# Decode stage of a hybrid trunk: separate step lists for three engines, another bank for the token turns, page numbers read before the buffer's wait

## The chip, the cores and the metric

One core of a Trainium2 chip runs the whole program in one launch. The metric is the device time in microseconds, median of several runs. All arithmetic is float32.

## The reference

Two layers over a prompt of 1024 tokens and 8 decode rows. Each layer projects once and splits the columns among three groups: latent attention (4 heads), an RWKV-7 time mixing (4 heads of 64, a 64x64 state per head) and a gated mixing of chunks. What matters here is the decode attention and the prompt's RWKV recurrence:

```python
# decode attention: 8 samples, 32 pages of 128 tokens each, latent width 256, rotary width 64
s_past = (einsum('blhr,bpr->bhlp', q_abs, ckv_past) + einsum('blhd,bpd->bhlp', q_pe, kpe_past)) * ATTN_SCALE
p = softmax(concatenate([s_past, s_new], -1))
o_lat = einsum('bhlp,bpr->blhr', p[..., :P], ckv_past) + einsum('bhlm,bmr->blhr', p[..., P:], ckv)

# RWKV-7, prompt: 1024 steps, run in the kernel as 16 chunks of 64
sa = einsum('bhvk,bhk->bhv', S, kk_t)
S = S * d_t - sa * b_t + v_t * k_t
o_t = einsum('bhvk,bhk->bhv', S, r_t)
```

The pages are gathered from a pool of 320 by `page_table`.

## The kernel before, in words

Each layer is a series of stages; the change is in one of them, the decode stage (lines 1328 to 1858). It does two independent things at once: the decode attention over the 8 samples' caches, and the chunked RWKV recurrence of the prompt. The engines have their own programs and meet at semaphores; each executes its program strictly in order.

**Attention.** A half-sample h (0 to 15, `NH`) is two page blocks q = 2h, 2h+1 of 8 pages each (`qpage`). The buffer holds six blocks (`QS`), that is three half-samples. SP loads a block with `load(sp, q)`: `reg_load` reads eight page numbers from the table into registers (line 401), and eight DMAs of 160 KB follow (line 404). From block 6 on SP first waits for `pg_free`, which TensorE raises when PV has read the block that lay there. For each h there are ten steps rb of 32 columns (`NB`): VectorE transposes the pages' columns in 32x32 blocks into one of four slots (`turn`, "T" below, line 1748), TensorE multiplies them with the queries in 32x32 tiles ("S", line 1589, 16 matmuls' passes). Then VectorE takes the maximum ("MX", lines 1807 to 1815), ScalarE the exponential ("EX", line 1690), TensorE transposes the probabilities into bank 4 ("PT", line 1598), ScalarE copies them out in four pieces (line 1700), and TensorE adds P V into bank 7 ("PV", line 1607). T waits for the step four before it to be used (`kt_used`), and for rb = 0 for its pages.

**Recurrence.** A pair p of chunks goes with the half-samples 2p and 2p+1. `prepare(p, n)` needs nothing of the state: MA and AK build the products inside a chunk; X1, Y1 to X5, Y5 invert a triangular 64x64 matrix in five levels (TensorE X, a copy of ScalarE, TensorE Y, an addition and a transpose of VectorE, then the next X; all in 32x32 tiles in bank 5); TA and TB transpose the token rows (b, k and v) in bank 6, from where ScalarE copies them. `follow(p - 1, n)` carries the state of the pair before: Z, U, H for each chunk c = 0, 1 and OO for the output, all in bank 6, each waiting for a copy or an addition of the one before. Z, U, H, OO and MA, AK are in 64x64 tiles, PT, TA, TB in 128x128, PV in 128x32.

**The order.** One list, `plan`, is written out by rule and walked by TensorE, ScalarE and VectorE alike; each picks the entries that concern it. "T" has no entries of its own: VectorE turns step n + 2 where the list has S of step n. For a pair the list gives TensorE this order (first digit of S: the half-sample of the pair; PT- and PV- belong to the half-sample before the pair):

```
S00 S01 MA Z0 S02 S03 PT- X1 U0 S04 S05 PV- Y1 H0 S06 S07 X2 Z1 S08 S09 Y2 U1 X3
S10 S11 H1 Y3 S12 S13 PT0 OO X4 S14 S15 PV0 AK Y4 S16 S17 TA X5 S18 S19 TB Y5
```

MX0 and EX0 stand between Y2, U1 and X3, MX1 and EX1 around Y5. TA waits for `ak_done`, because both use bank 6, and TB for `ta_done`.

Of the kernel before, what the change touches and what calls it, by code (L numbers as in the profile page):

```python
# [99 lines left out]
def bass_hybrid_trunk(nc, a):  # L100
    with ExitStack() as ctx:
# [92 lines left out]
        with nc.Fori(0, DEPTH) as layer:  # L194
# [198 lines left out]
            sv_io = sem("sv_io")  # L393
            pg_in = [sem(f"pg_in{i}") for i in range(QS)]
            HB = (10328, 0, 5120)
            tab = lnb[0:1, 0:NS * PAGES].bitcast(I32)
            qpage = lambda q: RB[:, HB[q // 2 % 3] + q % 2 * QW:HB[q // 2 % 3] + (q % 2 + 1) * QW].rearrange("p (s c) -> p s c", c=KW)

            def load(sp, q):
                regs = [sp.alloc_register(f"page{q}_{j}") for j in range(8)]  # L400
                sp.reg_load(regs, tab[:, 8 * q:8 * q + 8])
                for j, r in enumerate(regs):
                    page = sp.snap(r, donate=True)
                    sp.dma_start(qpage(q)[:, j], a["cache"][lay, bass.ds(page, 1), :, 0:KW].rearrange("l o p c -> (l o p) c")).then_inc(pg_in[q % QS], 16)
# [135 lines left out]
            with nc.Block() as block:  # L540
# [517 lines left out]
                def _(dve):  # L1058
# [229 lines left out]
                    for what, n, x in plan:  # L1288
# [40 lines left out]
            s_kn = sem("s_kn")  # L1329
            pg_free = sem("pg_free")  # L1330
            kt_used = sem("kt_used")
# [71 lines left out]

            STEPS = ["MA", "Z0", "X1", "U0", "Y1", "H0", "X2", "Z1", "Y2", "U1", "X3", "H1", "Y3", "OO",
                     "X4", "AK", "Y4", "TA", "X5", "TB", "Y5"]
            chain = ("Z", "U", "H", "O")


            plan = []
            for h in range(NH):  # L1410
                mine = [("rw", n) for n in (STEPS[0:11] if h % 2 == 0 else STEPS[11:])]
                for rb in range(0, NB, 2):
                    plan += [(h, "S", rb), (h, "S", rb + 1)]
                    if rb == 2 and h:
                        plan.append((h - 1, "PT", 0))
                    if rb == 4 and h:
                        plan.append((h - 1, "PV", 0))
                    if rb < 8:
                        plan += [(h // 2, *mine.pop(0)), (h // 2, *mine.pop(0))]
                rest = [(h // 2, *x) for x in mine]  # L1420
                plan += rest[:1] + [(h, "MX", 0)] + rest[1:2] + [(h, "EX", 0)] + rest[2:]
            plan += [(NH - 1, "PT", 0), (NS, "rw", "Z0"), (NH - 1, "PV", 0), (0, "FC", 1), (NS, "rw", "U0"), (0, "FC", 2), (NS, "rw", "H0"),
                     (0, "FC", 3), (NS, "rw", "Z1"), (0, "FC", 4), (NS, "rw", "U1"), (0, "FC", 5), (NS, "rw", "H1"), (0, "FC", 6),
                     (NS, "rw", "OO")]

            with nc.Block() as block:
                @block.sync
                def _(sp):
# [23 lines left out]
                def _(pe):  # L1452
# [4 lines left out]
                    def prepare(p, n):  # L1457
# [19 lines left out]
                        elif n == "TA":  # L1477
                            pe.wait_ge(ak_done, p + 1)
                            for f in range(2):
                                pe.transpose(PB[:, 6, f * P:(f + 1) * P], A2[:, f, p * P:(p + 1) * P], ident)  # L1480
                            for f in range(2):
                                mm = pe.transpose(PB[:, 6, (2 + f) * P:(3 + f) * P], pT[:, 2 + f, p * P + 1:(p + 1) * P + 1], ident)
# [43 lines left out]
                    def follow(p, n):  # L1526
# [45 lines left out]

                    for h, what, g in plan:
                        if what == "rw" and g[0] in chain:
# [58 lines left out]
                def _(act):  # L1633
                    def prepare(p, n):
# [9 lines left out]
                        elif n == "TA":  # L1644
                            act.wait_ge(ta_full, p + 1)
                            t6 = PB[:, 6, :].rearrange("p (v f w k) -> p v f w k", v=2, f=2, w=2)
                            for c in range(2):
                                for w in range(2):
                                    op = act.activation(TOK[k][hp[w], 0:2, 2 * c:2 * c + 2, :], t6[hp[c], :, :, w, :], ACT.Identity)
                            op.then_inc(ta_done, 1)  # L1650
# [27 lines left out]

                    for h, what, g in plan:
                        if what == "rw" and g[0] in chain:  # L1680
# [57 lines left out]
                def _(dve):  # L1738
# [20 lines left out]
                    def prepare(p, n):  # L1759
                        k = p % 2  # L1760
                        B = PB[:, 5, :].rearrange("p (v d c) -> p v d c", v=2, d=4)
                        if n == "MA":
# [9 lines left out]
                            dve.drain()  # L1772
                            dve.transpose(Tm.rearrange("p d c -> p (d c)"), Tc.rearrange("p d c -> p (d c)")).then_inc(tm_done, 1)
                            levels(2, LEVELS).then_inc(bm_done, 1)
                        elif n == "AK":
                            dve.wait_ge(ak_full, p + 1)
# [20 lines left out]
                    for h, what, g in plan:  # L1797
# [386 lines left out]
```

## Time and profile before

| what | value |
|---|---|
| median of 3 runs | 2040.42 us (2036.16 to 2041.38) |
| profiled execution, its own time | 2037.07 us |
| its span | 2035.4 us |
| TensorE busy | 1865.2 us (92%) |
| VectorE busy | 895.6 us (44%) |
| ScalarE busy | 494.7 us (24%) |
| page loads (line 404) | 512 of 160 KB, 2.6 us median from issue to landing |
| first and last S (line 1589) | 625.0 to 1871.6 us |

The busy shares are over the whole program. In the 40 slices of the page (51 us each) the decode stage lies in slices 13 to 17 for layer 0 and 33 to 37 for layer 1, where VectorE's digits are 6 to 7 and the DMA queues move 150 to 190 GB/s. A matmul's end is modelled, and float32 matmuls appear as two instructions each, so that one S group (8 matmuls) is 16 rows of the trace.

### The profile page before, as it was taken

The numbers are of one execution on the slowest core, as the hardware profiler recorded it, in microseconds if no ns is written. First come the engines' busy times: TensorE is split into PE (matmuls) and PEld (weight loads), VectorE is DVE, ScalarE is ACT, GpSimd is POOL, SyncE is SP. The second block draws the span as 40 slices with busy tenths as digits, with TensorE's granted clock in tenths as the row PEclk, the third lists the DMA queues.
The fourth block names the chain that finished last, engine by engine and source line by source line (L and its number), as shares of the span: only waits on it lengthen the run. The fifth ranks groups of instructions, "written<-read, shape, count | busy, mean of one in ns | idle before, by whom it ended". The sixth has DMA issues, their size and how long they took to land. (4 is left out here: it accounts for less than half of the span.)

```text
span 2035.4 us, 45818 instructions
## 1 busy us (share of the span) xinstructions
PE 1865.2 (92%) x19360; PEld 1164.3 (57%) x19360; DVE 895.6 (44%) x1984; ACT 494.7 (24%) x1164; POOL 172.6 (8%) x158
## 2 busy tenths in 40 slices
PE   4899999999987999899949999999999879998898
PEld 2565676666654666654326656766666546665543
DVE  2024134222766676654230340332318577775542
ACT  3111012222412333311131110222224123333201
POOL 0010000011334000000000100000212240000000
PEclk9899999999999999979989999999999899999899
DMA  9500000000205666341075001010001166562411
GB/s 388 207 11 27 21 21 32 21 21 13 59 26 159 185 188 180 109 178 42 32 301 213 0 27 32 11 32 22 21 22 50 28 186 186 176 186 83 178 42 42
DMA packets 103927, 191.18 MB, mean 94 GB/s; under 512 B 17162, under 2 KB 87260, under 8 KB 100004
## 3 DMA queue, kind: packets, MB, share of 16 engines
q1 hardware_dynamic: 103716, 188.19, 27.9%
q8 instruction: 154, 2.52, 0.5%
q14 instruction: 57, 0.47, 0.1%
HBM read 175.41 MB, written 21.19 MB: 97 GB/s over the span
## 5 line engine op out<-in xcount | busy, mean ns | idle before, releaser
L771 PE MATMUL PB<-RB,R 128*128 128x344 f32 x1632 | 496.1, 457 | 0.0
L771 PEld LDWEIGHTS PB<-RB,R 128*128 128x128 f32 x1632 | 303.7, 191 | 159.6 <-issue 19.7
L1946 PE MATMUL PB<-RB,R 128*128 128x512 f32 x512 | 221.2, 593 | 0.0
L1589 PE MATMUL PB<-WUQ,Q 32*32 32x256 f32 x5120 | 191.0, 385 | 14.7 <-DVE WUQ L1748 9.4
L1748 DVE STREAM_TRANSPOSE WUQ<-RB 128x512 f32<-128x512 f32 x316 | 197.0, 676 | 5.5 <-DMA RB<-in_cache 5.3
L1946 PEld LDWEIGHTS PB<-RB,R 128*128 128x128 f32 x512 | 97.0, 190 | 120.8 <-issue 118.6
L931 ACT ACTIVATE R<-PB 128x344 f32<-128x344 f32 x90 | 41.2, 457 | 423.4 <-PE PB L771 423.4
L1184 DVE TENSOR_TENSOR PB<-PB,CST 128x128 f32<-128x128 f32 x64 | 18.8, 294 | 226.3 <-PE PB L791 226.3
L1589 PEld LDWEIGHTS PB<-WUQ,Q 32*32 32x32 f32 x5120 | 90.0, 104 | 46.0 <-DVE WUQ L1748 23.1
L619 PE MATMUL PB<-RB,R 128*128 128x344 f32 x288 | 88.5, 472 | 10.8 <-PEq L225 10.8
L619 PEld LDWEIGHTS PB<-RB,R 128*128 128x128 f32 x288 | 57.1, 199 | 41.4 <-issue 14.8
L246 PE MATMUL PB<-R,WUQ 128*32 128x512 f32 x192 | 33.5, 667 | 49.2 <-DMA R<-in_w_ada 49.2
L1066 DVE COPY R<-PB 128x320 f32<-128x320 f32 x16 | 7.9, 491 | 149.7 <-PE PB L630 149.7
L788 PE MATMUL PB<-RB 128*128 128x128 f32 (+2 forms) x192 | 71.5, 495 | 0.0
L630 PE MATMUL PB<-RB 128*128 128x320 f32 x256 | 69.2, 432 | 0.0
L1607 PE MATMUL PB<-RB 128*32 128x256 f32 x1024 | 67.4, 404 | 1.9 <-ACT RB L1700 1.9
L2041 POOL TENSOR_TENSOR sm<-sm,small 128x1 f32<-128x1 f32 (+1 forms) x18 | 9.9, 550 | 698.6 <-DVE sm L2073 698.6
L942 ACT ACTIVATE R<-PB,sm,small 128x128 f32<-128x128 f32 (+3 forms) x64 | 53.2, 832 | 56.8 <-DVE sm L1188 56.2
L760 PE MATMUL PB<-R,RB 128*128 128x256 f32 x256 | 61.1, 383 | 0.0
L630 PEld LDWEIGHTS PB<-RB 128*128 128x128 f32 x256 | 48.6, 190 | 20.3
L1700 ACT ACTIVATE RB<-PB 64x256 f32<-64x256 f32 x128 | 48.3, 378 | 39.1 <-PE PB L1598 37.8
L2015 ACT ACTIVATE RB<-PB 128x1024 f32<-128x1024 f32 x16 | 16.3, 1021 | 161.2 <-PE PB L1946 161.2
(355 smaller groups left out, 2619.6 us busy)
## 6 DMA issues: line engine op xcount, KB each, us to landing
RB<-in_cache SPq DMA_DIRECT2D x512, 160.0 KB, 2.6
R<-in_w_ada SPq DMA_DIRECT2D x16, 1536.0 KB, 17.4
R<-in_w_in SPq DMA_DIRECT2D x44, 512.0 KB, 3.7
RB<-in_w_out SPq DMA_DIRECT2D x8, 1024.0 KB, 9.9
RB<-out_x_stream SPq DMA_DIRECT2D x2, 4096.0 KB
out_x_stream<-RB SPq DMA_DIRECT2D x16, 512.0 KB
RB<-in_x_prompt SPq DMA_DIRECT2D x1, 4096.0 KB
RB<-in_w_kv SPq DMA_DIRECT2D x2, 1280.0 KB, 5.6
```

Source lines behind the costliest of these rows:

```text
L619: mm = pe.matmul(bigbank(n)[:, c, :], ring[:, i % 4, k, :], hT[:, k, c * CH:(c + 1) * CH], start=(k == 0), stop=(k == KT - 1))
L630: mm = pe.matmul(smlbank("kv", t)[:, 0:KVW], hT[:, k, cols(t)], wkv_in[:, k, :], start=(k == 0), stop=(k == KT - 1))
L760: mm = pe.matmul(jobbank(j)[:, 0:256].rearrange("p (w c) -> p w c", w=2), hT[:, k, cols(c)], w2, start=(k == 0), stop=(k == KT - 1))
L771: mm = pe.matmul(jobbank(j)[:, 0:CH], ring[:, blkno[n] % 4, k, :], hT[:, k, chunk(c)], start=(k == 0), stop=(k == KT - 1))
L788: pe.matmul(sbank(2 * u + e)[:, c:c + w], qT[:, h, i * P:(i + 1) * P], kT[:, h, c:c + w], start=True, stop=False)
L931: act.activation(to, jobbank(j)[:, 0:CH], fn).then_inc(pj_free[j % 2], 1)
L942: act.activation(pbuf(n), sbank(n), ACT.Exp, bias=nbr[:, n:n + 1], scale=scq[:, i:i + 1], accum_out=Lr[:, n:n + 1]).then_inc(ex_done, 1)
L1589: mm = pe.matmul(PB[qp[o], 2 * (h % 2) + q % 2, 0:256], Q4[qp[q], g, :], k[qp[q], c], start=(g == 0), stop=(g == NB - 1), skip_group_check ...
L1607: mm = pe.matmul(PB[qp[c], 7, f * KVL:(f + 1) * KVL], PT[:, s, 32 * c:32 * c + 32], qpage(q)[:, (4 * s + c) % 8, RP:RP + KVL], start=(h == ...
L1700: op = act.activation(PT[hp[w], :, e * 64:(e + 1) * 64], t4[hp[e], :, w, :], ACT.Identity)
L1748: op = dve.transpose(KTr[:, n % 4], pages[:, :, fcol(rb):fcol(rb) + 32])
L1946: mm = pe.matmul(PB[0:n, 2 * (t % 2) + hf, :], mixT[:, k, cols(t)], wo[:, k, hf * 512:(hf + 1) * 512], start=(k == 0), stop=(k == 5))
```

## The change

SP's `load` reads the page numbers first and waits for the buffer afterwards. The common `plan` is replaced by a list for each engine, written out as words and expanded over the pairs. The word T gives VectorE's turns places of their own; LV is the second part of MA's levels, D a drain, and G0 and G1 are the scaling of the state for the next chunk, taken out of H0 and H1, with drains only in the last pair. Z0 now stands ahead of MA, PT- stands between U0 and H0, X1 stands behind PV-, S groups stand alone at seven places, and TB stands ahead of X5. TA's transposes go to bank 4, where the probabilities are turned, and no longer to bank 6: TA waits for `pp_done` of the pair's first half-sample, PT of the odd half-sample waits for `ta_done`, TB for `ak_done`, and Z also for `ta_done`.

```diff
-            def load(sp, q):
+            def load(sp, q, freed=0):
                 regs = [sp.alloc_register(f"page{q}_{j}") for j in range(8)]
                 sp.reg_load(regs, tab[:, 8 * q:8 * q + 8])
+                if freed:
+                    sp.wait_ge(pg_free, freed)
...
+            chain = ("Z", "U", "H", "G", "O")
+            PE_PAIR = (
+                "S00 S01 Z0 MA U0 PT- S02 H0 S03 S04 PV- X1 S05 Y1 S06 S07 Z1 S08 S09 U1 X2 S10 H1 Y2 S11 PT0 S12 OO "
+                "X3 PV0 Y3 S13 S14 S15 X4 AK TA Y4 S16 S17 TB S18 X5 S19 Y5"
+            ).split()
+            DVE_PAIR = (
+                "T02 T03 T04 MA T05 T06 H0 LV T07 T08 T09 Y1 T10 MX0 T11 G0 T12 D H1 Y2 T13 T14 T15 G1 T16 Y3 T17 T18 "
+                "T19 AK Y4 T20 T21 MX1"
+            ).split()
+            ACT_PAIR = (
+                "Z0 U0 PT- MA X1 Z1 U1 X2 EX0 PT0 OO X3 X4 TA X5 TB Y5 EX1"
+            ).split()
...
                     for q in range(4, 2 * NH):
-                        if q >= QS:
-                            sp.wait_ge(pg_free, q - QS + 1)
-                        load(sp, q)
+                        load(sp, q, max(q - QS + 1, 0))
...
                         elif n == "TA":
-                            pe.wait_ge(ak_done, p + 1)
+                            pe.wait_ge(pp_done, 2 * p + 1)
                             for f in range(2):
-                                pe.transpose(PB[:, 6, f * P:(f + 1) * P], A2[:, f, p * P:(p + 1) * P], ident)
+                                pe.transpose(PB[:, 4, f * P:(f + 1) * P], A2[:, f, p * P:(p + 1) * P], ident)
...
                         elif n == "TB":
-                            pe.wait_ge(ta_done, p + 1)
+                            pe.wait_ge(ak_done, p + 1)
...
                         if n[0] == "Z":
+                            pe.wait_ge(ta_done, p + 1)
                             pe.wait_ge(tb_done, p + 1)
...
                             if h:
                                 pe.wait_ge(pp_done, h)
+                            if h % 2:
+                                pe.wait_ge(ta_done, h // 2 + 1)
...
+                        elif n[0] == "G":
+                            i = 2 * p + int(n[1])
                             if i + 1 < NCH:
-                                dve.drain()
+                                if p == NS - 1:
+                                    dve.drain()
                                 dve.tensor_tensor(Sg, S0[:, (i + 1) % 4], ecol[:, :, i + 1:i + 2].broadcast_to([P, 2, 64]), ALU.mult)
-
-                    for h, what, g in plan:
+                                if p == NS - 1:
+                                    dve.drain()
+
+                    for h, what, g in pair_plan(DVE_PAIR):
...
-                        elif what == "S":
-                            if NB * h + g + 2 < NB * NH:
-                                turn(NB * h + g + 2)
+                        elif what == "T":
+                            turn(NB * h + g)
```

`pair_plan(words)` expands the words for p = 0 to 7, drops what lies outside the half-samples, and appends `TAIL`, the same end as before with G0 added behind H0.

## Rows read from the trace of the kernel before

**Rows 1.** Timeline of TensorE, 743 to 776 us: start, length, work, idle before it.
```profile
744.44 1.09 PE L1467 MATMUL PB<-RB 64*64 64x128 f32 x16 [0.45 <-ACT R L1661]
...
746.95 0.66 PE L1598 MATMUL PB<-CST,grow 128*128 128x128 f32 x4
748.01 0.45 PE L1515 MATMUL PB<-RB 32*32 32x32 f32 x32 [0.41 <-DVE RB L1773]
748.40 0.45 PE L1549 MATMUL PB<-RB,R 64*64 64x64 f32 x8
...
750.26 1.93 PE L1607 MATMUL PB<-RB 128*32 128x256 f32 x32
...
752.51 0.33 PE L1556 MATMUL PB<-R 64*64 64x64 f32 x4
...
753.12 1.09 PE L1589 MATMUL PB<-WUQ,Q 32*32 32x256 f32 x32
754.01 0.54 PE L1515 MATMUL PB<-RB 32*32 32x32 f32 x32
...
756.44 0.45 PE L1549 MATMUL PB<-RB,R 64*64 64x64 f32 x8
757.30 0.45 PE L1515 MATMUL PB<-RB 32*32 32x32 f32 x32 [0.42 <-DVE RB L1783]
757.58 1.14 PE L1589 MATMUL PB<-WUQ,Q 32*32 32x256 f32 x32
758.66 0.33 PE L1556 MATMUL PB<-R 64*64 64x64 f32 x4
...
759.77 0.45 PE L1522 MATMUL PB<-RB 32*32 32x32 f32 x32 [0.29 <-ACT RB L1664]
...
761.12 0.66 PE L1598 MATMUL PB<-CST,grow 128*128 128x128 f32 x4
761.71 0.33 PE L1565 MATMUL PB<-R 64*64 64x64 f32 x4
...
771.17 0.44 PE L1487 MATMUL PB<-CST,R 128*128 128x128 f32 x2 [0.35 <-ACT R L1649]
...
771.81 1.14 PE L1589 MATMUL PB<-WUQ,Q 32*32 32x256 f32 x31
773.40 1.09 PE L1467 MATMUL PB<-RB 64*64 64x128 f32 x16 [0.45 <-ACT R L1661]
```

**Rows 2.** Timeline of TensorE's weight loads: the second S group ahead of PV.
```profile
749.66 0.18 PEld L1589 LDWEIGHTS PB<-WUQ,Q 32*32 32x32 f32 x16 [0.41 <-DVE WUQ L1748]
```

**Rows 3.** Timeline of VectorE: the end of the first pair, then a pair's start.
```profile
650.46 1.30 DVE L1748 STREAM_TRANSPOSE WUQ<-RB 128x512 f32<-128x512 f32 x2 [2.20 <-DMA RB<-in_cache]
...
742.24 0.65 DVE L1808 TENSOR_REDUCE sm<-PB 128x1 f32<-128x512 f32 x1
...
743.72 1.29 DVE L1748 STREAM_TRANSPOSE WUQ<-RB 128x512 f32<-128x512 f32 x2
745.58 0.35 DVE L1764 TENSOR_SCALAR RB<-PB,CST 128x128 f32<-128x128 f32 x1 [0.56 <-PE PB L1467]
...
748.32 2.48 DVE L1748 STREAM_TRANSPOSE WUQ<-RB 128x512 f32<-128x512 f32 x4
```

**Rows 4.** Timeline of ScalarE in the same pair.
```profile
754.61 0.28 ACT L1664 ACTIVATE RB<-PB 128x128 f32<-128x128 f32 x1 [4.95 <-PE PB L1515]
...
759.45 0.27 ACT L1664 ACTIVATE RB<-PB 128x128 f32<-128x128 f32 x1
...
773.25 0.68 ACT L1690 ACTIVATE grow<-PB,sm 128x512 f32<-128x512 f32 x1
```

**Rows 5.** SP: lengths of line 404 and 401 (min/median/max ns), and waits, 640 to 880 us.
```profile
L404 SPq DMA_DIRECT2D RB<-in_cache x512: 332/333/1782, 547.8 to 1849.9; - x171
L401 SPq TENSOR_LOAD <-lnb x64: 520/525/772, 546.8 to 1844.2; - x64
SPq L401 <- PE PB L1607: 27.9, 12, 3.5
```

**Rows 6.** Windows behind the stage: TensorE, loads, VectorE, ScalarE, GpSimd, clock, DMA share, GB/s.
```profile
880.00:900.00 20.00, 18.00 (x69) 12.75 (x68) 7.99 (x19) 6.19 (x10) 0.00 (x0) 0.69 0.91 354
```

More of the change, by code:

```diff
@@ L394, in bass_hybrid_trunk @@
             pg_in = [sem(f"pg_in{i}") for i in range(QS)]
+            pg_free = sem("pg_free")
             HB = (10328, 0, 5120)
@@ L1329, in bass_hybrid_trunk @@
             s_kn = sem("s_kn")
-            pg_free = sem("pg_free")
             kt_used = sem("kt_used")
@@ L1402, in bass_hybrid_trunk @@
             fcol = lambda rb: RP + 32 * rb if rb < 8 else 32 * (rb - 8)
[L1404 to L1421, printed above, removed]
@@ L1422, in bass_hybrid_trunk @@
-            plan += [(NH - 1, "PT", 0), (NS, "rw", "Z0"), (NH - 1, "PV", 0), (0, "FC", 1), (NS, "rw", "U0"), (0, "FC", 2), (NS, "rw", "H0"),
-                     (0, "FC", 3), (NS, "rw", "Z1"), (0, "FC", 4), (NS, "rw", "U1"), (0, "FC", 5), (NS, "rw", "H1"), (0, "FC", 6),
-                     (NS, "rw", "OO")]
+            chain = ("Z", "U", "H", "G", "O")
[3 more added lines that the diff above has]
+            ).split()
@@ new lines, in bass_hybrid_trunk, with pair_plan @@
+            DVE_PAIR = (
[5 more added lines that the diff above has]
+            ).split()
+            def pair_plan(words):
+                out = []
+                for p in range(NS):
+                    for w in words:
+                        if w[0] in "ST" and w[1] in "012":
+                            out.append((2 * p + int(w[1]), w[0], int(w[2])))
+                        elif w[:2] in ("PT", "PV", "MX", "EX"):
+                            out.append((2 * p - 1 if w[2] == "-" else 2 * p + int(w[2]), w[:2], 0))
+                        else:
+                            out.append((p, "rw", w))
+                return [x for x in out if 0 <= x[0] < NH] + TAIL
@@ L1426, in bass_hybrid_trunk @@
+            TAIL = [(NH - 1, "PT", 0), (NS, "rw", "Z0"), (NH - 1, "PV", 0), (0, "FC", 1), (NS, "rw", "U0"), (0, "FC", 2), (NS, "rw", "H0"),
+                    (NS, "rw", "G0"), (0, "FC", 3), (NS, "rw", "Z1"), (0, "FC", 4), (NS, "rw", "U1"), (0, "FC", 5), (NS, "rw", "H1"),
+                    (0, "FC", 6), (NS, "rw", "OO")]
             with nc.Block() as block:
@@ L1477, in prepare @@
                         elif n == "TA":
-                            pe.wait_ge(ak_done, p + 1)
+                            pe.wait_ge(pp_done, 2 * p + 1)
                             for f in range(2):
-                                pe.transpose(PB[:, 6, f * P:(f + 1) * P], A2[:, f, p * P:(p + 1) * P], ident)
+                                pe.transpose(PB[:, 4, f * P:(f + 1) * P], A2[:, f, p * P:(p + 1) * P], ident)
                             for f in range(2):
-                                mm = pe.transpose(PB[:, 6, (2 + f) * P:(3 + f) * P], pT[:, 2 + f, p * P + 1:(p + 1) * P + 1], ident)
+                                mm = pe.transpose(PB[:, 4, (2 + f) * P:(3 + f) * P], pT[:, 2 + f, p * P + 1:(p + 1) * P + 1], ident)
                             mm.then_inc(ta_full, 1)
                         elif n == "TB":
-                            pe.wait_ge(ta_done, p + 1)
+                            pe.wait_ge(ak_done, p + 1)
                             for f in range(2):
@@ L1571, in follow @@
                             mm.then_inc(oo_full, 1)
-                    for h, what, g in plan:
+                    for h, what, g in pair_plan(PE_PAIR):
                         if what == "rw" and g[0] in chain:
@@ L1645, in prepare @@
                             act.wait_ge(ta_full, p + 1)
-                            t6 = PB[:, 6, :].rearrange("p (v f w k) -> p v f w k", v=2, f=2, w=2)
+                            t4 = PB[:, 4, :].rearrange("p (v f w k) -> p v f w k", v=2, f=2, w=2)
                             for c in range(2):
                                 for w in range(2):
-                                    op = act.activation(TOK[k][hp[w], 0:2, 2 * c:2 * c + 2, :], t6[hp[c], :, :, w, :], ACT.Identity)
+                                    op = act.activation(TOK[k][hp[w], 0:2, 2 * c:2 * c + 2, :], t4[hp[c], :, :, w, :], ACT.Identity)
                             op.then_inc(ta_done, 1)
@@ L1677, in follow @@
                             act.activation(A3[:, :, p * P:(p + 1) * P], PB[:, 6, 0:2 * P].rearrange("p (f t) -> p f t", f=2), ACT.Identity).then_inc(oo_done, 1)
-                    for h, what, g in plan:
+                    for h, what, g in pair_plan(ACT_PAIR):
                         if what == "rw" and g[0] in chain:
@@ L1773, in prepare @@
                             dve.transpose(Tm.rearrange("p d c -> p (d c)"), Tc.rearrange("p d c -> p (d c)")).then_inc(tm_done, 1)
+                        elif n == "LV":
                             levels(2, LEVELS).then_inc(bm_done, 1)
+                        elif n == "D":
+                            dve.drain()
                         elif n == "AK":
@@ L1792, in follow @@
                             op.then_inc(st_done, 1)
+                        elif n[0] == "G":
+                            i = 2 * p + int(n[1])
                             if i + 1 < NCH:
-                                dve.drain()
+                                if p == NS - 1:
+                                    dve.drain()
                                 dve.tensor_tensor(Sg, S0[:, (i + 1) % 4], ecol[:, :, i + 1:i + 2].broadcast_to([P, 2, 64]), ALU.mult)
-                    for h, what, g in plan:
+                                if p == NS - 1:
+                                    dve.drain()
+                    for h, what, g in pair_plan(DVE_PAIR):
                         if what == "rw" and g[0] in chain:
```

## The prediction

> **What bounds the kernel now.** I read the page first (busy shares, the 40 slices), then the waits between 640 and 880 us, then the timelines of TensorE, VectorE and ScalarE over one pair of half-samples, 744 to 773 us, where nothing of the start or the end of the stage mixes in. The reader is to see there that the decode stage (about 625 to 881 us in layer 0, 1635 to 1893 us in layer 1) repeats one pattern eight times per layer. Its period is the distance between two MA groups on TensorE: 773.40 - 744.44 = 28.96 us [rows 1]. TensorE executes its own list in order, and its groups follow each other without a hole except at a few places; ScalarE has a pause of 4.95 us in it [rows 4] and VectorE another while it waits for Y1 and AK. So the stage is TensorE's work plus the holes that the order of its list makes.
>
> I price the holes from start to start, against the same group where it does not wait [rows 1]. (a) S18 S19 and then Y5, S00, S01 up to MA: 771.81 to 773.40 is 1.59 us, two S groups ahead of a 64x64 group normally take 758.66 - 757.58 = 1.08, so 0.51. (b) PT: 748.01 - 746.95 = 1.06 against 761.71 - 761.12 = 0.59, so 0.47. (c) U0 S04 S05: 750.26 - 748.40 = 1.86 against 1.08 and a U of 0.38, so 0.40 (no U is seen without a wait: I take it between half an H, 0.31, and its own duration, 0.45). (d) U1: 757.30 - 756.44 = 0.86 against 0.38, so 0.48. (e) H1: 759.77 - 758.66 = 1.11 against 753.12 - 752.51 = 0.61, so 0.50. (f) TB: idle 0.35 us for TA's copies, as its row says. Sum 2.71 us, and the work without holes is 28.96 - 2.71 = 26.25 us.
>
> **The change part by part.** The matmuls, copies and transposes of a pair stay the same in number, shape and operands; only their order, TA's bank and some waits differ. So TensorE's 26.25 us stay, apart from the seams. Two S groups take 754.01 - 753.12 = 0.89 us in front of another 32x32 group, 0.445 each, and a lone S in front of PV, a group of another tile size, takes 750.26 - 749.66 = 0.60 [rows 1, 2]. The difference, 0.15, is a seam. Counting the runs of 32x32 groups (S, X, Y) that end in another size, the old order has 12 per pair and the new one 11: work 26.10 us.
>
> The Trainium skill ("TensorEngine Tiling (Array Packing)", Tiling Modes, Key Properties) says that each change of tiling mode drains the engine, so by it every change of size counts, also 64x64 to 128x128. That would be 26 changes before and 24 after, another 0.15 us per pair, some 2 us over the kernel; the rows here price only exits from 32x32, and I keep to them.
>
> Now the new holes. I walk the new lists with X5 of a pair's end at 0, with these prices: one turn T 2.48/4 = 0.62; MX to the next instruction 743.72 - 742.24 = 1.48; MA with its levels 748.32 - 745.58 = 2.74 [rows 3]; a copy of X 0.28 and EX 0.68 with some 0.1 for its sum [rows 4]; the other groups by their start distances in the same timeline of TensorE (Z 0.57, MA 0.93, PV 1.86, OO 1.54, AK 1.02, TA 0.59, TB 0.36).
> - X5 to Y5. X5's result is there after 0.5, its copy ends at 0.85, Y5 can start at 0.9; S19 between them covers up to about 0.6. Hole 0.3 (before, TA's copies stood in front of X5's).
> - S00 S01 at 1.15, Z0 at 2.2, MA at 2.8. MA wants the copy after Y5, which ScalarE does behind TB's four copies: ready at 2.6. Hole (a) goes, because Z0 now stands in front of MA. Late next is z_done for U0: ScalarE's Z0 copy now stands behind EX1, which waits for MX1, which waits for S19 (done at 0.85). 0.9 + 1.55 + 0.05 + 0.78 + 0.05 + 0.28 gives 3.6 and U0 wants it at 3.7. No hole, but only 0.1 of cover; without it every tenth counts.
> - U0, PT, S02, H0, S03, S04, PV. H0's copy of U0 is covered by PT and S02 (1.2 us against 0.85). PT's four copies end at 6.3, PV starts at 6.95. VectorE does T02 to T04, MA, T05, T06: MA's transpose is out at 6.6 and X1, moved behind PV, wants it at 8.8. Holes (b) and (c) go.
> - X1, S05, Y1. One S (0.45) and X1 itself cover 0.7 of 0.9: hole 0.2.
> - S06 S07 Z1 S08 S09 U1 X2 S10 H1 Y2 S11. Y1's transpose is out at 11.15, X2 wants it at 13.05: hole (d) goes. S10 and H1 (1.2 us) cover X2's copy: hole (e) goes. MX0 waits for S09 (12.8); T11 behind it is out at 15.0 and S11 wants it at 14.8: hole 0.2.
> - PT0 S12 OO X3 PV0. EX0's result at 15.2 and PT0 at 15.6; H1's state is out at 16.3 (behind MX0, T11, G0, T12) and OO wants it at 16.8; X3 at 18.3 has Y2's transpose since 16.8; PT0's copies end at 17.9, PV0 starts at 18.8. No hole.
> - Y3 S13 S14 S15 X4 AK TA Y4 S16 S17 TB S18. Y3's transpose is out at 21.9, X4 wants it at 22.2. TA's bank is free since 17.9. TB's wait on AK ends at 24.4, wanted at 25.6; TB no longer waits for TA's copies (the rest of f). X5 wants Y4's transpose (25.5) at 26.4. No hole.
> Added waits on TensorE (ta_done in front of both Z groups and of the odd PT) are long satisfied. Their cost isn't in the trace; between 0 and the 0.05 us that lies between the end of a releasing copy and the group that it releases (the copy of L1664 for Y3 ends at 759.45 + 0.27 and Y3 starts at 759.77, [rows 1, 4]) I take 0.05 each, 0.15 a pair. Taking the drains out of VectorE's G steps gives less than 0.2 us on an engine that has 3 us of pauses left: nothing.
>
> New period: 26.10 + 0.3 + 0.2 + 0.2 + 0.15 = 26.95 by the sum, in which X5's and Y5's own time is partly counted twice with their holes, and 26.4 by adding the starts of the walk directly. I take 26.6, between them: 2.36 us less per pair.
>
> **The page loads.** SP issues 32 loads a pair. One issue is 0.33 us and now and then up to 1.78; a read of eight page numbers takes 0.52, and SP waits 27.9 us for PV in layer 0, in 12 of the waits [rows 5]. So the two bursts of 16 fill 28.96 - 27.9/8 = 25.5 us of a pair, 12.7 each. In the new order PV- frees its first buffer at 7.9, the burst ends at 20.6 and the pages land 2.6 later (the median in the page's list of loads), 23.2; T20 wants them at 25.4. PV0 frees at 19.8, behind the first burst at 20.6: landed at 35.9, which is 9.3 of the next pair against T10 at 11.1. About 2 us of cover both times. Reading the numbers ahead of the wait takes 0.5 us off each even burst, behind that cover: worth nothing while it lasts.
>
> **Start and end of the stage.** T20 of the first pair waits for page block 5 until 650.46 [rows 3], and block 5 is issued without waiting for any buffer. The first pair cannot end earlier: gain 0. The tail behind the last S19 is a chain (MX, EX, PT, copies, PV, the final combination) with the same steps: 0, with two drains more, under 0.2. So seven pairs per layer gain, 14 x 2.36 = 33 us.
>
> **Sum.** The profiled execution took 2037.07 us (span 2035.4). 2037.1 - 33 = 2004.1. The median of the timed runs stands 3.35 us above the profiled one, so I forecast 2007.4, about 2007 us, 1.6% less.
>
> **Rivals.**
> 1. The page loads become the bound. For: SP is busy 25.5 of 28.96 us, more than any other engine but TensorE, and bursts without their pause would fill 25.5 of the new 26.6. Against: 1.1 us is left, and landing has 2 us. If each issue's queueing grows so that a burst takes 13.6 us, the period is 27.2 and the gain 14 x 1.75 = 25 us: 2016.
> 2. The seams eat the gain. The new list has seven lone S groups where the old has none; I priced them by one row. If each costs 0.2 more (a full new fill, half of S's own 0.44), 1.4 us of the 2.36 goes: 14 x 0.96 = 13 us, 2027.
> 3. Slower than before. MX now stands in front of things that TensorE wants next, at two places: MX1, EX1, Z0's copy for U0 (cover 0.1) and MX0, T11 for S11 (none). A delay d of the maxima costs 2d a pair; from d = 1.2 us the gain is gone, and at 1.48 us (VectorE held up in front of it by as much as one more MX) the kernel is 14 x 0.6 = 8 us slower: 2048. Against it: MX starts within 0.1 us of its last S today.
> 4. The clock. TensorE's granted clock is 0.69 between 880 and 900 us [rows 6], that is between its levels of 1.2 and 2.4 GHz, behind the tail of the stage, in which TensorE mostly waits. Where the low stretch falls on the projection it costs time at half speed; shifted by a few us in each layer it can give or take 5 us. This widens the range of every case and is not a case of its own.
>
> **Numbers.** Forecast 0.62 (own range 1998 to 2016); rival 1 0.12; rival 2 0.15; rival 3 0.05; 0.06 for all holes closed (14 x 2.71 = 38 us, 2002, and with the clock below 1998). Within 0.3% (6 us, about what runs of this kernel can tell from no change) lies the upper part of rival 2 and the start of 3: 0.07. Range 1998 to 2024. Faster 0.88, same 0.07, slower 0.05.
>
> **What would show it.** In the profile after: the MA distance near 26.6 us in the middle of the stage; no idle of TensorE in front of MA, X3, Y3 or TB; small idle in front of Y5, Y1 and S11; VectorE never idle for DMA behind the first pair; SP's waits for PV down to some 10 us a layer. The forecast is wrong if U0 or S11 waits for over 0.5 us a pair, if a lone S takes over 0.7 us, or if VectorE waits for pages in several pairs.

## The result and the profile after

The changed kernel takes 2014.93 us (median of 4 runs) against 2040.90 us for the kernel before: the ratio is 0.9875, 95% interval 0.9852 to 0.9897, so 26 us or 1.25% less. A second group of runs gave 2014.23 us against 2039.85 us (0.988, 0.9851 to 0.9908). Forecast were 2007 us and 33 us less; the direction and the range held, and a fifth of the gain is missing. One of the first four runs took 2745.53 us, in the slow state of the chip (granted clock 0.65 instead of 0.97); it is left out of the ratio, though not of the median.

The profiled execution has a span of 2012.6 us, 22.8 less than before. Of these the decode stage gives 18.0: from its first S to its last, it was 234.3 us in layer 0 and 236.7 in layer 1, and is 225.6 and 227.4. The remaining 4.8 us lie in stages that the change doesn't touch, 2.6 of them before the stage of layer 0 begins: the first S stands at 622.4 instead of 625.0 us, with the same matmuls at a mean granted clock of 0.99 instead of 0.98. I don't count them for the change. Of the 33 us forecast for the stage, the one profile shows 18, then, and the timed runs some 21 to 26.

Busy rows of the page after, TensorE, its loads, VectorE and ScalarE, are nearly those of before, as they must be:

```profile
PE 1864.4 (93%) x19360; PEld 1165.3 (58%) x19360; DVE 896.8 (45%) x1984; ACT 497.4 (25%) x1164; POOL 172.1 (9%) x158
```

The distances between the MA groups of TensorE (the period that the forecast put at 26.6 us) are, in us:

```
pair            1->2   2->3   3->4   4->5   5->6   6->7   7->8
before, layer 0 26.35  33.77  29.32  28.94  28.96  30.29  29.44
after,  layer 0 27.84  32.20  27.25  28.10  29.06  28.84  26.25
before, layer 1 26.89  35.14  29.27  28.93  29.44  30.09  29.75
after,  layer 1 28.97  30.45  31.08  29.40  28.56  26.25  26.69
```

Two things stand there. Where nothing disturbs it, the new order runs at 26.25 us, even less than the walk's 26.4. And most pairs don't reach it: from the third on, seven of ten periods lie between 27.3 and 31.1 us. The forecast had asked for 26.6 us in the middle of the stage; that sign did not appear.

Here is the undisturbed pair, from the timeline of TensorE after (Z0 in front of MA, then as in the list):

```profile
796.73 1.04 PE L1475 MATMUL PB<-RB 64*64 64x128 f32 x16
797.61 0.40 PE L1558 MATMUL PB<-RB,R 64*64 64x64 f32 x8
797.93 0.66 PE L1609 MATMUL PB<-CST,grow 128*128 128x128 f32 x4
798.52 0.66 PE L1598 MATMUL PB<-WUQ,Q 32*32 32x256 f32 x16
799.11 0.33 PE L1565 MATMUL PB<-R 64*64 64x64 f32 x4
...
802.88 0.72 PE L1598 MATMUL PB<-WUQ,Q 32*32 32x256 f32 x16
803.47 0.45 PE L1530 MATMUL PB<-RB 32*32 32x32 f32 x32
...
806.83 0.45 PE L1523 MATMUL PB<-RB 32*32 32x32 f32 x32
807.11 0.72 PE L1598 MATMUL PB<-WUQ,Q 32*32 32x256 f32 x16
...
808.37 0.45 PE L1530 MATMUL PB<-RB 32*32 32x32 f32 x32
808.90 0.67 PE L1598 MATMUL PB<-WUQ,Q 32*32 32x256 f32 x16
...
814.47 0.45 PE L1530 MATMUL PB<-RB 32*32 32x32 f32 x32
814.75 1.58 PE L1598 MATMUL PB<-WUQ,Q 32*32 32x256 f32 x48
...
818.12 0.45 PE L1530 MATMUL PB<-RB 32*32 32x32 f32 x32
818.40 1.15 PE L1598 MATMUL PB<-WUQ,Q 32*32 32x256 f32 x32
819.47 0.44 PE L1495 MATMUL PB<-CST,R 128*128 128x128 f32 x2
...
820.32 0.32 PE L1502 MATMUL PB<-RB 32*32 32x32 f32 x10
...
822.47 0.33 PE L1547 MATMUL PB<-R 64*64 64x64 f32 x4
```

Between these rows TensorE never stands idle long enough for the trace to name a releaser. The lone S (02) takes 799.11 - 798.52 = 0.59, as [rows 2] had it. Two of the three holes that the forecast left show as slack from start to start: S05 to Y1 is 0.59 where an S in a run is 0.445 (0.15, forecast 0.2), Y2 to S11 is 0.53 where Y1 to S06 is 0.27 (0.26, forecast 0.2). The third, 0.3 in front of Y5, can't be read by itself, because X5, S19 and Y5 overlap in the trace; from X5 to Z0 it is 822.47 - 820.32 = 2.15, and 2.2 in the walk.

And here a disturbed pair, 738.8 to 767.9 us, 2.8 us longer:

```profile
749.24 0.33 PE L1523 MATMUL PB<-RB 32*32 32x32 f32 x16
749.84 0.33 PE L1523 MATMUL PB<-RB 32*32 32x32 f32 x16 [0.28 <-issue]
750.02 0.67 PE L1598 MATMUL PB<-WUQ,Q 32*32 32x256 f32 x16
...
757.28 0.43 PE L1530 MATMUL PB<-RB 32*32 32x32 f32 x27
758.06 0.22 PE L1530 MATMUL PB<-RB 32*32 32x32 f32 x3 [0.35 <-issue]
758.08 0.43 PE L1598 MATMUL PB<-WUQ,Q 32*32 32x256 f32 x5
...
761.50 0.38 PE L1530 MATMUL PB<-RB 32*32 32x32 f32 x23
762.34 0.23 PE L1530 MATMUL PB<-RB 32*32 32x32 f32 x4 [0.45 <-issue]
762.38 0.40 PE L1598 MATMUL PB<-WUQ,Q 32*32 32x256 f32 x1
...
763.41 0.44 PE L1495 MATMUL PB<-CST,R 128*128 128x128 f32 x2
...
766.36 1.08 PE L1598 MATMUL PB<-WUQ,Q 32*32 32x256 f32 x28 [0.42 <-issue]
767.37 0.33 PE L1547 MATMUL PB<-R 64*64 64x64 f32 x4
```

The reader is to see that TensorE stops inside its groups. X2 is one group of 32 instructions with waits only ahead of its first; its first 16 start at 749.24, the rest at 749.84, and the idle is "issue": nothing that the profile shows was waited for. From start to start against the undisturbed pair: X2 to S10 0.78 instead of 0.28, Y3 to S13 0.80 instead of 0.28, Y4 to S16 0.88 instead of 0.28, TB to Z0 3.96 instead of 3.00. These four breaks are 2.58 of the 2.81 us.

TensorE's instructions have a queue of their own on the page (q8, by its size). Of the page after, queues with packets, MB and share:

```profile
q1 hardware_dynamic: 103716, 188.19, 28.4%
q8 instruction: 154, 2.52, 0.5%
q14 instruction: 57, 0.47, 0.1%
```

154 packets for TensorE's 38,720 matmuls and loads are one for about 251 of them, 16 KB each. A pair has some 1,730, so seven refills a pair, one in 3.8 us at the new pace. That the breaks are refills that come late was a theory at this point.

The trace bears it out. These are TensorE's matmuls and loads from one resumption to a later one in the disturbed pair (the stretch, TensorE, loads, VectorE, ScalarE, GpSimd, clock, DMA share, GB/s):

```profile
749.84:758.06 8.22, 7.87 (x255) 5.22 (x256) 5.59 (x16) 3.23 (x9) 0.00 (x0) 1.00 0.67 194
758.06:762.34 4.28, 3.83 (x129) 3.05 (x130) 3.07 (x6) 1.00 (x3) 0.00 (x0) 1.00 0.57 169
762.34:766.36 4.02, 3.60 (x127) 1.82 (x128) 2.80 (x8) 2.37 (x10) 0.00 (x0) 1.00 0.81 241
```

That is 511, 259 and 255 instructions, two blocks of 256, one and one (what overlaps an edge counts on both sides). Numbered through in the order of their starts, waits included, 16 of the 17 gaps of over 0.35 us inside a group in pairs 3 to 6 of both layers stand at a multiple of 256 from one another within their layer. At each of the 22 block ends with a gap of over 0.25 us TensorE goes on 1.2 to 1.6 us after a 16 KB packet of q8 has ended.

The second loss is at the start. VectorE's waits for pages, in the timelines of VectorE after (first two pairs of layers 0 and 1):

```profile
647.62 1.30 DVE L1759 STREAM_TRANSPOSE WUQ<-RB 128x512 f32<-128x512 f32 x2 [3.84 <-DMA RB<-in_cache]
664.86 0.71 DVE L1759 STREAM_TRANSPOSE WUQ<-RB 128x512 f32<-128x512 f32 x1 [3.49 <-DMA RB<-in_cache]
```
```profile
1648.42 1.30 DVE L1759 STREAM_TRANSPOSE WUQ<-RB 128x512 f32<-128x512 f32 x2 [5.43 <-DMA RB<-in_cache]
1664.39 0.71 DVE L1759 STREAM_TRANSPOSE WUQ<-RB 128x512 f32<-128x512 f32 x1 [2.84 <-DMA RB<-in_cache]
```

The first of each is T20, which waited 2.20 us in [rows 3] and now waits longer because the first pair is quicker: that was forecast. The second is T30 in the second pair, for blocks 6 and 7, which had never waited.

SP's waits for PV between 640 and 860 us (total, times, longest), against the row of [rows 5]:

```profile
SPq L407 <- PE PB L1618: 17.2, 5, 4.9
```

### The profile page after: what moved, and what is told of

It reads as the page before. It is cut to its first block and busy times, and to the rows that moved or that the text cites. A ratio compares the mean times of both kernels' runs of the same rounds, so it can differ in the third digit from the quotient of the medians.

```text
span 2012.6 us, 45810 instructions
## 1 busy us (share of the span) xinstructions
PE 1864.4 (93%) x19360; PEld 1165.3 (58%) x19360; DVE 896.8 (45%) x1984; ACT 497.4 (25%) x1164; POOL 172.1 (9%) x158
## 3 DMA queue, kind: packets, MB, share of 16 engines
q8 instruction: 154, 2.52, 0.5%
## 5 line engine op out<-in xcount | busy, mean ns | idle before, releaser
L1598 PE MATMUL PB<-WUQ,Q 32*32 32x256 f32 x5120 | 200.2, 387 | 21.5 <-DVE WUQ L1759 12.9
L1759 DVE STREAM_TRANSPOSE WUQ<-RB 128x512 f32<-128x512 f32 x316 | 203.2, 680 | 18.5 <-DMA RB<-in_cache 15.6
```

The costliest lines, as they stand in the source:

```text
L1598: mm = pe.matmul(PB[qp[o], 2 * (h % 2) + q % 2, 0:256], Q4[qp[q], g, :], k[qp[q], c], start=(g == 0), stop=(g == NB - 1), skip_group_check ...
L1759: op = dve.transpose(KTr[:, n % 4], pages[:, :, fcol(rb):fcol(rb) + 32])
```

## The experiments

The theories: **F**, the refills of TensorE's instructions queue behind page packets and break its groups; **P**, only the late pages at the start keep the gain down; **S**, seams and hand-overs of the new order cost more than I walked.

**The changed kernel again.** No edit.

> The changed kernel as it is, beside the runs of this group on the same chip. Theories: F (instruction refills of TensorE queue behind the page packets and break groups in the middle), P (late pages in pairs 1 and 2 alone keep the gain down), S (the seams and hand-overs of the new order cost more than walked). All three expect 2015 us within 4 us, periods of 28 to 29 us while pages load and 26.3 us in the last ones.

Measured: 2014.23 us (0.988, 0.9851 to 0.9908). Its periods in pairs 3 to 7 are 28.62, 27.27, 28.73, 26.82, 26.26 us in layer 0 and 28.85, 29.39, 28.86, 26.38, 26.89 in layer 1.

**Thin page loads in the changed kernel.**

```diff
-sp.dma_start(qpage(q)[:, j], a["cache"][lay, bass.ds(page, 1), :, 0:KW]...)
+sp.dma_start(qpage(q)[:, j, 0:40], a["cache"][lay, bass.ds(page, 1), :, 0:40]...)
```

> The changed kernel, but each page load brings only 40 of a row's 320 columns (the scores are then of stale data; all instructions, waits and the number of loads stay). F: no breaks inside TensorE's groups any more, every period from the third pair on 26.2 to 26.6 us, and 12 periods gain 1 to 3 us each: about 2015 - 22 = 1993 us. P: only the two waits for pages go (15.6 us in the profile of the changed kernel): about 2000 us, periods in the middle still 28 to 29 us. S: nothing but those waits, the same periods.

Measured: 1997.11 us (0.9797, 0.9775 to 0.9818). The periods of pairs 3 to 7 are 26.42, 26.86, 26.67, 27.53, 26.26 and 26.43, 26.95, 26.72, 26.26, 26.56 us, mean 26.67. F stands, S falls, and P falls as the only cause: the same instructions with the same waits run close to the walked period as soon as the pages carry an eighth of the bytes. The waits for pages did not go (3.62 and 0.93 us in layer 0, 3.23 and 1.32 in layer 1), but they shrank from 15.6 to 9.1 us. In the profiles the seven periods of both layers are together 21.9 us shorter; 7.1 of it lie in the first two periods, where the waits for pages are, and 14.8 in the other five, where VectorE never waits for a page. So roughly two thirds of what the traffic costs are breaks, and up to a third is late pages.

**Thin page loads in the kernel before.** The same edit.

> The same thinning (40 of 320 columns per load) on the kernel before. F: its waits on semaphores leave the refills time to catch up, so it gains less: periods from 28.9 to 30.3 go to 28.5 to 28.9 us, with the pages' wait of 5.3 us about 2041 - 13 = 2028 us, and the distance to the changed kernel thinned alike grows to 30 to 37 us, near the walked 33. P or S: the distance stays 26 us or less.

Measured: 2032.74 us (0.9967, 0.9957 to 0.9977), 7 us less than before and not the 13 expected; the middle periods are 28.93 to 29.22 us in layer 0 and 28.93 to 29.45 in layer 1. The distance between the two kernels without the page traffic is 35.6 us, close to the 33 that were walked. The windows of four pairs (layer 0) say the same. One line for each kernel: the stretch, TensorE, loads, VectorE, ScalarE, GpSimd, clock, DMA share, GB/s; first the kernel before, then the changed one:

```profile
686.20:803.70 117.50, 108.20 (x3449) 73.22 (x3450) 84.75 (x209) 43.27 (x137) 0.00 (x0) 1.00 0.61 182
```
```profile
683.50:796.70 113.20, 109.27 (x3450) 72.96 (x3452) 85.90 (x210) 44.01 (x136) 0.00 (x0) 1.00 0.64 190
796.70:823.00 26.30, 26.21 (x872) 18.01 (x868) 20.26 (x51) 10.39 (x33) 0.00 (x0) 1.00 0.64 190
```

Then the kernel before with thin loads and the changed one with thin loads:

```profile
683.00:799.00 116.00, 106.68 (x3450) 72.97 (x3450) 84.75 (x209) 43.26 (x137) 0.00 (x0) 1.00 0.15 27
```
```profile
679.80:787.30 107.50, 106.35 (x3456) 72.23 (x3452) 86.27 (x211) 44.54 (x138) 0.00 (x0) 1.00 0.17 29
```

All four stretches hold the same four pairs (3450 matmul rows). In layer 0 the order is worth 116.0 - 107.5 = 8.5 us for four pairs without page traffic (forecast 9.4) and 117.5 - 113.2 = 4.3 with it: half. The traffic costs the old order 1.5 us in four pairs and the new one 5.7. The same four pairs of layer 1, from MA to MA, take 117.7 and 115.3 us with the traffic and 116.5 and 106.4 without: there the order gains 10.1 us without it and only 2.4 with it, and the traffic costs 1.3 and 8.9 us. (The changed kernel run again has 111.4 and 113.5, so one profile is good to some 2 us here.)

The trace also shows how. For each of the 54 blocks of 256 instructions in pairs 3 to 6 of both layers I took from it the gap in front of the block, the time from the start of the block before it to the start of the packet that brings it, and how long that packet takes (medians, us):

```
                      gaps over 0.25   their sum   packet starts after   packet takes
before                       6            2.9            1.16                1.06
before, thin                 0            0              0.83                1.08
changed                     22           15.9            1.37                1.11
changed, run again          21           14.4            1.42                0.98
changed, thin                3            2.2            0.91                1.07
```

The packet for a block starts only once the block before it has begun, and with the page traffic it starts 0.3 to 0.5 us later. It takes no longer itself. With the 1.2 us or more from its end to the first instruction, a block is ready some 3.7 us after the one before it began with the traffic, and 3.2 us without (an estimate, from these medians). TensorE needs 3.7 us for a block of the new order (median) and 4.25 for one of the old, in which its waits are included: the old order's waits leave the refills the time that the new one takes away. The gaps fall by 13.7 us from the changed kernel to the thin one, of 14.7 us by which these eight pairs get shorter.

**Half the bytes.** 160 of 320 columns per load, else as the thin one.

> The changed kernel with 160 of 320 columns per page load. F: the breaks depend on how much page traffic stands in the queues, so at half the bytes they are mostly gone: about 1997 us, near the thin one. If they depend on the number of loads or packets (which is unchanged) and not on bytes, 2010 us or more.

Measured: 1997.71 us (0.9804, 0.9779 to 0.9828), the same as with an eighth of the bytes. The number of page packets is the same in all three. So it is bytes that matter (or the time that a packet holds its engine, which falls with them: median 55, 32 and 14 ns), and between half and whole most of the loss comes about. In layer 1 some breaks remain (periods up to 28.14 us; 9 gaps with 4.8 us in all among the 54 blocks).

**The page numbers read late again.**

```diff
-                sp.reg_load(regs, tab[:, 8 * q:8 * q + 8])
                 if freed:
                     sp.wait_ge(pg_free, freed)
+                sp.reg_load(regs, tab[:, 8 * q:8 * q + 8])
```

> The changed kernel with the page numbers read behind the buffer's wait again. By the forecast the 0.5 us read lies behind some 2 us of cover: no difference, 2014 us within 3. Rival: SP is the bound from the second pair on, then 14 bursts begin 0.5 us later: 2014 + 7 = 2021 us.

Measured: 2015.90 us (0.9869, 0.9852 to 0.9885): no difference, as forecast. Its profiled execution is the longest of its four (span 2022.4), with breaks in nearly every pair, also in pairs 6 and 7 (28.86, 27.57; 29.52, 27.68), though TensorE's instructions are the same and its blocks end at the same places: which pair suffers is not fixed by the code alone.

**The bank alone, in the old order.** TA's transposes and copies in bank 4, TB waits for AK, as in the change; the common `plan` stays.

> The kernel before with one part of the change: TA's transposes and copies through bank 4, TB waits for AK instead of TA. Hole f goes (0.35 us of TensorE's idle, 0.49 from start to start, a pair): 14 x 0.4 = 6 us, 2034 us. Rival: TensorE meets Y5's copy (hole a) that much earlier and ScalarE, which still copies TA, X5, TB, Y5 in a row, hands nothing on sooner: then a grows by what f loses and the kernel stays at 2040 us.

Measured: 2038.57 us against 2042.48 (0.998, 0.9968 to 0.9992): 3.9 us, between the two expectations. TB's idle is gone, and with it a hole of 0.28 us opens in front of Y5 for ScalarE's copy of X5.

**The order alone, without the bank.**

```diff
                         elif n == "TA":
-                            pe.wait_ge(pp_done, 2 * p + 1)
+                            pe.wait_ge(ak_done, p + 1)
-                            ... PB[:, 4, ...]        # four transposes, and ScalarE's copies
+                            ... PB[:, 6, ...]
                         elif n == "TB":
-                            pe.wait_ge(ak_done, p + 1)
+                            pe.wait_ge(ta_done, p + 1)
```

> The changed kernel without the change of bank: TA and TB share bank 6 with AK as before, with the waits that this needs. In the new order TA follows AK at once and must wait for AK's product to be taken out (0.7 us), and TB follows TA's four copies 0.3 us too early: 1.0 us a pair, 14 pairs, 2015 + 14 = 2029 us. If these waits only take the place of breaks for refills (theory F: TensorE's refills catch up in any pause), about 2021 us. Rival: the bank was worth no more than in the old order (3.9 us there): 2019 us.

Measured: 2028.53 us (0.9952, 0.9933 to 0.997), 14 us above the changed kernel. Both waits have the size that was worked out, in the timeline of TensorE:

```profile
765.14 0.44 PE L1488 MATMUL PB<-CST,RB 128*128 128x128 f32 x2 [0.80 <-DVE R L1788]
767.44 0.44 PE L1495 MATMUL PB<-CST,R 128*128 128x128 f32 x2 [0.29 <-ACT R L1657]
```

By the medians the bank is worth 14 us in the new order and 4 us in the old: the two parts belong together, and the order alone gives 12 of the 26 us. The four runs lie far apart (2023.15 to 2032.3 us), so the 14 is rough. The profiled execution is the shortest of them, and in it some of the extra waits did take the place of breaks: its 54 blocks have 18 gaps with 9.4 us in all, where the changed kernel has 15.9 and 14.4.

**Z0 behind MA again.**

```diff
-                "S00 S01 Z0 MA U0 PT- S02 ...
+                "S00 S01 MA Z0 U0 PT- S02 ...
```

> The changed kernel with MA ahead of Z0 on TensorE, the rest of its order as it is. MA then waits for the copy of Y5 and U0 for Z0's copy with nothing between them. Forecast's prices: about 0.4 for MA and Z0 end to copy end 0.4 for U0: 0.8 us a pair, 14 pairs: 2014 + 11 = 2025 us. If the refills take whatever slack there is (F), part of the new waits is paid out of their breaks in the pairs with page traffic: 2014 + 5 = 2019 us.

Measured: 2027.82 us (0.993, 0.9914 to 0.9947), 13 us above the changed kernel, near the 11 us of the forecast's prices. U0 waits for Z0's copy in each of the 14 pairs, as priced:

```profile
747.06 0.45 PE L1558 MATMUL PB<-RB,R 64*64 64x64 f32 x8 [0.47 <-ACT RB L1681]
```

MA's wait is smaller than its price of 0.4: 1.0 us in six pairs. Gaps at block ends did not shrink for these waits (25 with 15.7 us in all among 54 blocks).

**Pages first.** Blocks 4 and 5 are issued right behind block 3, ahead of the sampled rows' state loads; the eight small loads of the new latents go behind block 31.

> The changed kernel with page blocks 4 and 5 issued right behind block 3 (ahead of the state loads of the sampled rows) and the eight loads of the new rows' latents behind the last page block. The waits for pages in pairs 1 and 2 (3.8 and 3.5 us in layer 0, 5.4 and 2.8 in layer 1) go but for what the GpSimd work, now later, takes from VectorE: 2014 - 12 = 2002 us. If the refills take it back in the pairs that now run closer to the loads: 2008 us.

Measured: 2014.40 us (0.9855, 0.983 to 0.9879): no gain that can be told. The wait of T20 shrinks to 0.61 us in layer 0 and goes in layer 1, and the first pair gets 2.6 and 2.7 us shorter, but T30 waits as before (3.26 and 3.11 us) and the second pair is 33.00 and 33.40 us instead of 31.73 and 31.36 (both against the changed kernel run again).

**No GpSimd arithmetic.** The chain of products and sums on the sampled rows' state is replaced by one copy.

> The changed kernel without GpSimd's arithmetic on the sampled rows' state (one copy stands for it; the sampled state's outputs are then not computed). If the two VectorE operations that take 1.3 to 1.9 us beside GpSimd in the second pair hold up the chain of that pair, the second period falls by 1.5 to 3 us per layer: 2015 - 5 = 2010 us. If the second pair is bound by its pages (wait of T30 for block 7) anyway, no change: 2014 us.

Measured: 2018.72 us (0.9899, 0.9883 to 0.9916), no gain. VectorE's operations that are longer beside GpSimd (one at 655.41 us in the profile after takes 1.20 us, and 0.29 at 686.40; 1.93 us at 656.21 in the kernel before) are not what bounds the second pair: without GpSimd's work T30 waits 3.12 and 4.39 us, and the second period is 31.05 and 32.16 us.

**State loads issued by ScalarE.** The six loads of the sampled rows' state, and `gsum` with them, move from SP's program to the head of ScalarE's, the new latents behind block 31.

> The changed kernel with the state loads of the sampled rows issued by ScalarE, which is idle at the start of the stage, and the new rows' latents behind the last page block; SP issues nothing but pages. GpSimd then starts as early as in the changed kernel, T20 of the first pair no longer waits (4 to 5 us a layer) and pair 2 doesn't grow as it did when GpSimd's work moved into it (1.3 and 2 us): 2015 - 8 = 2007 us. Rival: what is gained in pair 1 is only waited for at T30, whose pages depend on PV of the first half-sample: that PV comes earlier too, so I hold this for less likely; 2013 us.

Measured: 2011.55 us (0.9871, 0.9851 to 0.9892). The waits for pages fall from 15.6 us in four to 4.1 us in two, and the second period from 32.20 and 30.45 to 27.57 and 27.92 us. So SP's other loads at the start are what made the pages of the second pair late. Yet only some 3 us of this arrive, inside the noise: the first period is 28.85 us, and breaks are now in pairs 6 and 7 of layer 0 too (28.31 and 27.68 us). It is the fastest version that was run with the whole page loads, but its lead over the changed kernel isn't shown.

**More page loads at the end.** Four blocks more, into buffers that are done with.

```diff
+                    for q in range(2 * NH, 2 * NH + 4):
+                        load(sp, q, q - QS + 1)
+                    for q in range(2 * NH, 2 * NH + 4):
+                        sp.wait_ge(pg_in[q % QS], 128 * (q // QS + 1))
...
```

> The changed kernel with four more page blocks (32 loads) issued behind the last ones, into buffers that nobody reads any more and that nobody waits for but SP at its end. In the changed kernel the pairs from 796 us and from 1772 us on, which run beside no or little page traffic, take 26.25 to 26.7 us. F: the traffic alone makes breaks inside TensorE's groups there, and the last two periods of each layer that ran at 26.3 to 26.9 us go to 27.5 to 29 us: 2015 + 5 = 2020 us. Any theory in which late pages, seams or hand-overs make the longer periods of the middle: those periods stay at 26.3 to 26.9 us, 2015 us.

Measured: 2017.91 us (0.9888, 0.9871 to 0.9904). The last periods went from 26.26 and 26.89 to 28.09 and 27.90 us, with breaks; the ones before them (27.20 and 26.64) are near those of the changed kernel run again (26.82 and 26.38). I don't take this as a proof: the experiment rested on the idea that those pairs run beside little traffic, and they don't. The stretch of pair 7 has a DMA share of 0.65 and 196 GB/s in the changed kernel run again, and 0.63 and 188 GB/s here:

```profile
796.80:823.10 26.30, 26.21 (x872) 18.01 (x868) 20.88 (x53) 10.52 (x35) 0.00 (x0) 1.00 0.65 196
```
```profile
800.10:828.20 28.10, 27.08 (x870) 18.33 (x868) 20.69 (x52) 10.45 (x33) 0.00 (x0) 1.00 0.63 188
```

So page traffic is what makes breaks frequent (thin and half loads take nearly all of them away), but a pair can come through whole traffic without any. In the changed kernel's profile a break comes where two things meet: the block before it was a quick one (3.4 us of work against 4.2 in front of the other block ends, medians of pairs 3 to 6), and the packet started late (1.63 us after that block's start against 1.22). What delays the packet's start beside the page loads the runs don't show.

## Why the prediction was right, and where it fell short

**The holes (a) to (f) and the walk: right.** The undisturbed period is 26.25 us, the thin mean 26.67, forecast 26.4 to 26.6. Holes (a) to (e) are gone, TB's idle (f) too; the remaining ones before Y1 and S11 have their forecast size. Two single steps, taken back one at a time, cost about what was worked out: Z0 ahead of MA 13 us (expected 11), the bank 14 us (expected 14, with runs 9 us apart).

**The seams: right.** At the four places where a lone S comes before a group of another tile size it takes 0.59, 0.64, 0.60 and 0.59 us in the undisturbed pair (S02, S10, S11, S12), as the one row said, so rival 2 did not happen. The other three of the seven stand before X or Y groups and end no run. The Trainium skill's rule ("TensorEngine Tiling (Array Packing)", Key Properties) would have given 2 us more; the runs here can't tell 2 us.

**TensorE's supply of instructions: the step that failed.** The sentence "So TensorE's 26.25 us stay, apart from the seams" took the groups as solid. They are, as long as the next block of instructions is there. In the profile of before the breaks were to be seen (the period of 30.29 us holds one of 0.8 us at 793.92), and I took the pair 744 to 773 us, in which there are none, for all. At the old pace refills came one in 4.2 us, with waits between them; at 3.8 us without waits the traffic costs the new order 5.7 - 1.5 = 4.2 us more than the old one in four pairs of layer 0 and 8.9 - 1.3 = 7.6 us in layer 1, half and three quarters of the order's gain there. The Trainium skill ("Runtime: NRT & Kernel Launch", Instruction fetch mechanics) says that a 16 KB block holds 256 instructions, which the 154 packets of 2.52 MB bear out, and that crossing a block's end is mostly hidden; beside 180 to 190 GB/s of page loads it was not: 22 of 54 block ends cost 15.9 us.

**The page loads: right in the middle, wrong in the second pair; the smaller second step that failed.** From the third pair on VectorE never waits for a page in the profile after, and SP still has pauses (17.2 us in layer 0, in 5 waits; I had said some 10). The first pair gained nothing, as forecast. But I counted seven gaining pairs and used the cover of a steady pair (2 us) for the second one as well. Its blocks 6 and 7 depend on the first pair's PV and on SP, which at that time still carries state and latent loads, and T30 waited 3.5 and 2.8 us; with those loads off SP it no longer waited. The first two periods together gave 0.1 us in layer 0 and 2.6 us in layer 1 instead of 2.4 each; part of that is MA's own move in the pair.

**Reading the page numbers ahead: right**, worth nothing that can be measured (2015.9 against 2014.9 and 2014.2 us).

**Rivals.** The price of rival 1 (2016 us) is near what was measured, but mostly by another mechanism: behind the second pair the page loads did not bound the stage by arriving late, they slowed the supply of instructions. None of the rivals had that, and the 0.62 chance went to a forecast in which TensorE never stops inside a group. Rivals 2 and 3 did not occur: MX0 starts 0.1 us behind its last S, and U0 has no hole in the undisturbed pair. Of rival 4 nothing clear can be said: the stretch before the first S is 2.6 us shorter at a clock of 0.99 instead of 0.98, and I count that neither for nor against the change.

## What to carry to other kernels

An in-order engine with many small instructions has a second input beside its semaphores: its instruction stream. Before counting holes as gain, look for idle inside a group, where no wait stands, and compare several periods, not the cleanest one; where there is such idle, the pauses that an order leaves may be what the refills live on. To size it, cut the bytes of the parallel transfers and keep all instructions: the difference is what traffic costs. And two edits that look separate can belong together: the bank alone gave 4 us and the order alone 12, both together 26.

## What the runs showed of the hardware

- TensorE's instructions come in packets of 16 KB, one per 256 instructions (251 of them matmuls and weight loads, on average). Beside page loads of 1280-byte rows at 180 to 190 GB/s, TensorE stopped 0.3 to 2.1 us inside groups, up to four times in 29 us; in pairs 3 to 6 of the two layers 16 of 17 stops of over 0.35 us stand at the end of such a block. With rows of 640 or 160 bytes, the same number of packets, most stops went (22 of 54 block ends before, 9 and 3 then), and the kernel took 17 us less of 2014.
- A block's packet starts about 1.4 us after the block before it began beside the page loads and 0.9 us after it with thin ones, takes 1.0 to 1.1 us in both (medians), and at a stop TensorE goes on 1.2 to 1.6 us after its end.
- The page traffic, stops and late pages together, costs the order with 2.7 us of waits per pair 7 us over the kernel and the order with few waits 17 us.
- The same traffic does not stop TensorE in every pair: 26.25 and 29.06 us for the same instructions at 190 and 179 GB/s within 60 us of each other.
